# A mixture-of-experts layer on Trainium2: the rows beyond 128 of an expert by plain four-byte products in column tiles, from raw weights

## The reference

```python
scores = sigmoid(xf @ w_router)                 # pick 8 experts of 64 for each token
for each block of rows of one expert e:
    h  = silu(xb @ w_gate[e]) * (xb @ w_up[e])  # 1024 -> 256
    yb = (h @ w_down[e]) * rw                   # 256 -> 1024, weighted
    acc[rows] += yb
shared = (silu(xf @ ws_gate) * (xf @ ws_up)) @ ws_down
x = layer_norm(ALPHA * x + acc + shared)
```

## Time and profile before

| | |
|---|---|
| median of 3 runs | 1641.52 us (1641.01 to 1644.18) |
| the profiled execution | 1632.95 us, its span 1631.3 us |
| TensorE busy | 1574.2 us, 97% of the span |
| DVE, ACT, POOL busy | 73%, 63%, 31% |
| mean granted clock of TensorE | 0.979 |
| DMA | 368.63 MB, mean 226 GB/s |

### The profile page before, as it was taken

One profiled execution on the slowest core, in us unless ns is written; L12 is line 12 of the kernel. 1 busy time (PEld: TensorE's weight loads), 2 busy tenths in 40 slices (PEclk: granted clock), 3 DMA queues, 4 the chain that ended last, 5 costly groups with the idle time before them and its releaser, 6 DMA issues.

```text
span 1631.3 us, 32225 instructions
## 1 busy us (share of the span) xinstructions
PE 1574.2 (97%) x8262; PEld 1310.3 (80%) x8263; DVE 1183.2 (73%) x2038; ACT 1033.3 (63%) x1709; POOL 505.7 (31%) x495
## 2 busy tenths in 40 slices
PE   6999999999999999899999999999999999999987
PEld 6997888888887788788888888788888888888864
DVE  4215777777777788838777888767876787888856
ACT  3215666666666645427667877766776777877855
POOL 0000000000000135532544454543554455454426
PEclk9999999999999999899999999999999999999995
DMA  7223222212223524568999999999998999999987
GB/s 247 91 82 96 67 59 65 71 45 71 58 65 111 185 108 170 196 218 315 318 303 309 304 363 360 329 289 263 331 322 276 286 356 326 348 365 370 366 252 283
DMA packets 161319, 368.63 MB, mean 226 GB/s; under 512 B 53008, under 2 KB 73488, under 8 KB 161264
## 3 DMA queue, kind: packets, MB, share of 16 engines
q1 hardware_dynamic: 136272, 284.21, 49.9%
q0 software_dynamic: 24992, 83.73, 19.8%
HBM read 294.39 MB, written 65.11 MB: 220 GB/s over the span
## 4 chain that ended last, share of the span: by engine, by line
PE 78%; DVE 7%; issue 4%; ACT 3%; DMA 3%; ACTq 2%; POOL 1%; SPq 0%; DVEq 0%; POOLq 0%
PE bank_pair L1032 6%; PE bank_pair L1035 6%; PE bank_pair L1038 6%; PE q_ps L91 4%; PE out_ps L923 4%; PE q_ps L93 4%; PE q_ps L92 4%; PE k_ps L901 4%; PE out_ps L1091 4%; PE out_ps L1092 3%; PE q_ps L1022 3%; PE k_ps L1059 3%; PE k_ps L1060 2%; PE k_ps L1067 2%; DVE gu_lo L1926 2%
## 5 line engine op out<-in xcount | busy, mean ns | idle before, releaser
L1926 DVE TENSOR_TENSOR gu_lo<-raw_gu,gu_hi 128x1024 fp32r<-128x1024 f32 x260 | 306.4, 1219 | 28.7 <-ACT gu_hi L1404 28.7
L1404 ACT CAST gu_hi<-raw_gu 128x1024 fp32r<-128x1024 f32 x260 | 253.3, 1050 | 6.0 <-DMA raw_gu<-in_moe_w_up_dram 6.0
L1032 PE MATMUL bank_pair<-gu_hi,xb_hi 128*128 128x512 f32 x576 | 235.5, 409 | 5.4 <-DVE gu_lo L1926 4.2
L1035 PE MATMUL bank_pair<-gu_lo,xb_hi 128*128 128x512 f32 x576 | 229.1, 398 | 0.0
L689 POOL DMA_INDIRECT sums_scratch<-ys,sidx x63 | 119.8, 1902 | 151.7 <-DMA sums_scratch<-ys,sidx 110.6
L1926 DVE TENSOR_TENSOR dn_lo<-raw_dn,dn_hi 128x1024 fp32r<-128x1024 f32 x130 | 152.6, 1213 | 2.2 <-ACT dn_hi L1404 1.7
L1038 PE MATMUL bank_pair<-gu_hi,xb_lo 128*128 128x512 f32 x576 | 142.7, 390 | 0.0
L1032 PEld LDWEIGHTS bank_pair<-gu_hi,xb_hi 128*128 128x128 f32 x576 | 111.5, 194 | 29.5 <-issue 6.5
L1309 ACT CAST pt_hi<-k_ps 128x512 fp32r<-128x512 f32 (+1 forms) x192 | 85.9, 482 | 74.2 <-PE k_ps L901 73.4
L620 POOL IOTA e<- 128x64 f32 x1 | 0.2, 185 | 426.6 <-DVE xs L1722 426.6
L1404 ACT CAST dn_hi<-raw_dn 128x1024 fp32r<-128x1024 f32 x130 | 130.0, 1051 | 3.2 <-DMA raw_dn<-in_moe_w_down_dram 3.2
(11 more groups left out here) (306 smaller groups left out, 3971.5 us busy)
## 6 DMA issues: line engine op xcount, KB each, us to landing
raw_gu<-in_moe_w_gate_dram SPq DMA_DIRECT2D x128, 512.0 KB, 6.6
raw_gu<-in_moe_w_up_dram SPq DMA_DIRECT2D x128, 512.0 KB, 9.1
raw_dn<-in_moe_w_down_dram SPq DMA_DIRECT2D x128, 512.0 KB, 8.9
wqk<-in_fox_w_in_dram SPq DMA_DIRECT2D x66, 128.0 KB, 2.4
v_scratch<-v_out SPq DMA_DIRECT2D x32, 256.0 KB, 2.8
va<-v_scratch SPq DMA_DIRECT2D x16, 512.0 KB, 4.7
fin<-sums_scratch SPq DMA_DIRECT2D x16, 512.0 KB, 9.0
xs<-in_x_dram SPq DMA_DIRECT2D x8, 512.0 KB, 7.8
```

The lines of the kernel that those rows point to most:

```text
L1032: i = pe.matmul(o3, xb_hi[s][:, c], g_hi[:, :, c], start=c == 0, stop=False, skip_group_check=True)
L1035: pe.matmul(o3, xb_hi[s][:, c], g_lo[:, :, c], start=False, stop=False, skip_group_check=True)
L1404: a.copy(hi, raw).then_inc(S[done], 1)
L1926: dve.tensor_tensor(lo, raw, hi, ALU.subtract).then_inc(S[lo_ok], 1)
```

## The change

The further blocks are multiplied in the plain four-byte type by the raw weights, without split halves. A 32-row block is 32 columns wide as a stationary operand, so four products go to four 32-column tiles of the array, whose results land in partitions 0, 32, 64 and 96 (`x_tile(j)`): for gate/up the tiles are gate and up of the even and of the odd chunks, 16 products of 256 columns; for down they are the two halves of the columns by the two chunks, 4 products of 512 columns. ACT copies and DVE adds the partial sums. `xo` and `ho` are a quarter as wide, and their low halves are gone; so are `hh` (now in `sg`), `gu_x` and `ys2`, which lie in unused partitions of `x_rows2`.

As the further products read the raw weights, these must stay. There is a third raw gate/up buffer; the buffer is `raw_place(s)`. SP waits besides for `started` (gate/up) and `downed` (down). The loops go by six, the least common count of pairs and threes; experts 0, 1, 62 and 63 stand outside. The table `tab` is kept in two-byte integers, cast by POOL from a copy that lies in the third up buffer. Some tiles of the final stage are moved, with three waits for it (`downed` ahead of the sums of tiles 2 to 7, `started` ahead of `tokens`, `c_const` ahead of set 3).

```diff
-            raw_gu = [sb(f"raw_gu{i}", [P, 2, DC, FF], c=m) for i in range(2)]
+            raw_gu = [[sb(f"raw_{n}{i}", [P, DC, FF], c=m) for n in ("gate", "up")] for i in range(2)]
...
+            raw_gu.append([third_gate, sb("raw_up2", [P, DC, FF], c=m)])
...
+        def raw_place(s):
+
+            return s if s < 2 else (0, 2, 1)[(s - 2) % 3]
...
+        ROUND = 6
+        ROUNDS = (E - 4) // ROUND
...
+            def next_gate_up(s, place):
+
+                if place > 3:
+                    sp.wait_ge(S["started"], SH + s - 2)
+                    stand(sp)
+                load_gate_up(place, *(w[ds(s - 1, 1)].rearrange("o k n -> (o k) n") for w in (w_gate, w_up)),
                              lambda k: sp.wait_ge(S["g_lo_ok"], G_PIECES * (s - 2) + k + 1))
 
+            def next_down(s, place):
+                if place > 2:
+                    sp.wait_ge(S["downed"], SH + s - 2)
+                    stand(sp)
+                load_down(place % 2, w_down[ds(s - 1, 1)].rearrange("o k n -> (o k) n"),
                           lambda k: sp.wait_ge(S["d_lo_ok"], D_PIECES * (s - 2) + k + 1))
...
+            sp.wait_ge(S["c_const"], 11)
+            next_gate_up(3, 3)
+            with sp.Fori(0, ROUNDS) as i:
+                for u in range(ROUND):
+                    next_gate_up(ROUND * i + (u + 4), u + 4)
+                    next_down(ROUND * i + (u + 3), u + 3)
...
+            sp.wait_ge(S["downed"], SH + E)
             for t in range(2, TT):
                 load_sums(1, t)
...
+                        g.tensor_copy(tab[:], tab_in).then_inc(S["c_const"], 1)
...
-                for c in range(DC):
-                    pe.matmul(o3, xo[:, c], g_hi[:, :, c], start=c == 0, stop=False, skip_group_check=True)
-                    i = pe.matmul(o3, xo[:, c], g_lo[:, :, c], start=False, stop=c == DC - 1, skip_group_check=True)
+                for c in range(0, DC, 2):
+                    for j in range(4):
+                        i = pe.matmul(out_ps[x_tile(j), BANK:BANK + FF], xo[:, c + j // 2], raw[j % 2][:, c + j // 2], start=c == 0,
+                                      stop=c == DC - 2, skip_group_check=True)
...
-                for r in HALVES:
-                    for c in range(FC):
-                        pe.matmul(out_ps[:, r], ho[:, c], d_hi[:, c, r], start=c == 0, stop=False, skip_group_check=True)
-                        i = pe.matmul(out_ps[:, r], ho[:, c], d_lo[:, c, r], start=False, stop=c == FC - 1, skip_group_check=True)
+                for j in range(4):
+                    c, half = (j // 2, j % 2) if by_rows else (j % 2, j // 2)
+                    i = pe.matmul(out_ps[x_tile(j), BANK:T], ho[:, c], raw[:, c, HALVES[half]], start=True, stop=True, skip_group_check=True)
...
+                a.copy(gu_x[:, 0:FF], out_ps[x_tile(2), BANK:BANK + FF]).then_inc(S["x_half"], 1)
+                a.copy(gu_x[:, FF:2 * FF], out_ps[x_tile(3), BANK:BANK + FF]).then_inc(S["x_up_half"], 1)
...
+                a.copy(y_half, out_ps[2 * XR:P, BANK:T]).then_inc(S["x_y_half"], 1)
...
+                dve.tensor_tensor(gu_x[:, 0:FF], out_ps[x_tile(0), BANK:BANK + FF], gu_x[:, 0:FF], ALU.add).then_inc(S["x_sum"], 1)
...
+                dve.tensor_tensor(ys_x[:, BANK:D], out_ps[x_tile(1), BANK:T], ys_x[:, BANK:D], ALU.add)
+                dve.tensor_tensor(ys_x[:, 0:BANK], out_ps[x_tile(0), BANK:T], y_half[0:XR], ALU.add).then_inc(S["x_scaled"], 1)
```

More of the change, by code:

```diff
@@ L347, in build, with g_piece, d_piece, x_tile @@
         ds = bass.ds
[L349 to L353 removed]
+        def raw_place(s):
+            return s if s < 2 else (0, 2, 1)[(s - 2) % 3]
+        def g_piece(s, k):
+            c = slice((k % 2) * 4, (k % 2) * 4 + 4)
+            return (raw_gu[raw_place(s)][k // 2][:, c], split[s % 2][0][:, k // 2, c], split[s % 2][1][:, k // 2, c])
+        def d_piece(s, k):
+            w = s % 2
             return tuple(a[:, k, :] for a in (raw_dn[w], split[w][2], split[w][3]))
+        def x_tile(j):
+            return slice(j * XR, (j + 1) * XR)
+        ROUND = 6
+        ROUNDS = (E - 4) // ROUND
         def v_bank(n, j, w):
@@ L548, in _ @@
                 elif b == 5:
-                    next_gate_up(2, 0)
+                    next_gate_up(2, 2)
                 elif b == 6:
-                    next_down(2, 0)
+                    next_down(2, 2)
             sp.wait_ge(S["listed"], 16 * TT * TOP_K)
@@ L554, in _ @@
             sp.wait_ge(S["extra_ok"], 2)
-            sp.dma_start(tab[:], tab_dram.rearrange("(p n) o -> p (n o)", p=P)).then_inc(S["c_loads"], 16)
-            next_gate_up(3, 1)
-            with sp.Fori(0, E // 2 - 2) as i:
-                for par in range(2):
-                    next_gate_up(2 * i + (par + 4), par)
-                    next_down(2 * i + (par + 3), 1 - par)
-            next_gate_up(E, 0)
-            next_down(E - 1, 1)
-            next_down(E, 0)
+            sp.dma_start(tab_in, tab_dram.rearrange("(p n) o -> p (n o)", p=P)).then_inc(S["c_loads"], 16)
+            sp.wait_ge(S["c_const"], 11)
[4 more added lines that the diff above has]
+                    next_down(ROUND * i + (u + 3), u + 3)
+            next_gate_up(E, E)
+            next_down(E - 1, E - 1)
+            next_down(E, E)
             def load_sums(j, t):
@@ L1170, in _, with expert @@
                     logits(TT - 1)
-            def expert(e, par, last=False):
+            def expert(e, u, last=False):
+                par = u % 2
                 w = 1 - par
@@ L1224, in expert @@
                 return xi, nx
-            with pe.Fori(0, E // 2 - 1) as i:
-                for par in range(2):
-                    expert(2 * i + par, par)
-            expert(E - 2, 0)
-            expert(E - 1, 1, last=True)
+            for e in range(2):
+                expert(e, e)
+            with pe.Fori(0, ROUNDS) as i:
+                for u in range(2, ROUND + 2):
+                    expert(ROUND * i + u, u)
+            expert(E - 2, E - 2)
+            expert(E - 1, E - 1, last=True)
         @block.scalar
@@ L1522, in load_counts, with expert @@
                 return [act.value_load(earlier[0:1, ds(e + k, 1)], min_val=0, max_val=E * TAB_BLOCKS) for k in range(4)]
-            def expert(e, par, pos, counts):
+            def expert(e, u, pos, counts):
+                par = u % 2
                 m = SH + e
@@ L1597, in _ @@
             expert(1, 1, "", counts)
-            with act.Fori(1, E // 2 - 1) as i:
-                counts = load_counts(2 * i)
-                for par in range(2):
-                    expert(2 * i + par, par, "", counts)
+            with act.Fori(0, ROUNDS) as i:
+                for u in range(2, ROUND + 2):
+                    if u % 2 == 0:
+                        counts = load_counts(ROUND * i + u)
+                    expert(ROUND * i + u, u, "", counts)
             counts = load_counts(E - 2)
-            expert(E - 2, 0, "", counts)
-            expert(E - 1, 1, "last", counts)
+            expert(E - 2, E - 2, "", counts)
+            expert(E - 1, E - 1, "last", counts)
             for t in range(TT):
@@ L2014, in load_counts, with expert @@
                 return [dve.value_load(earlier[0:1, ds(e + k, 1)], min_val=0, max_val=E * TAB_BLOCKS) for k in range(4)]
-            def expert(e, par, counts, last=False):
+            def expert(e, u, counts, last=False):
+                par = u % 2
                 m = SH + e
```

186 lines of the change are left out of this document (93 added, 93 removed).

## The result

The changed kernel takes 1787.04 us (median of 4 runs, 1785.11 to 1792.73) against 1641.76 for the kernel before beside it (4 runs): a ratio of 1.089, 95% interval 1.086 to 1.092. The forecast was 1585, with 0.11 for slower. Its profiled execution has a span of 1785.6 us.

What follows compares the result with a forecast made beforehand. TensorE, busy 97% of the span, was taken as the bound, with DMA limiting short intervals after the change. The stage's -52 us and the ends' -5 made -57: 1576 profiled, 1585 median, range 1550 to 1620.

Steps and rivals of the forecast that it cites:

- Bigger loop bodies: Loops of six experts: fewer branches, 30 to 10, between -10 and +10 us, taken as 0.
- The products: Further gate/up on TensorE in four overlapping column tiles: 1.96 us, 1.68 saved; further down 1.10 us, 0.84 saved; 31 times each.
- own: 15 intervals between turn_h starts holding the expert's own further gate/up: from 14.18 to 12.50 us, TensorE-bound.
- both: 15 intervals holding the previous block's tail and the expert's own block: from 16.56 to 14.04 us, TensorE-bound.
- tail: 15 intervals holding the previous expert's block's turn h and down: TensorE 11.73 to 10.89 us, DMA-bound at 11.95.
- The weights' queue: SP's weight loads, called the deciding step: bursts each interval at 365 GB/s limit the stage's gain to -52 us.
- short interval: 17 intervals between turn_h starts without further block: 9.35 us on TensorE, DMA-bound at 11.6 us, +32.7 in all.
- without carry: Stage sum if no burst may end late into the next interval: -34.7 us; late bursts add about 17.
- The bursts of SP's waits: Rival: weight queue runs dry within each interval, so its mean rate falls; 1640 to 1700 us, chance 0.09.
- Ends: Last intervals and final stage: 4 us off from less DMA backlog, 1 us from the last block.
- small waits pile up: Rival: new small waits, such as POOL's adds, take 1 us from each of 45 intervals; 1605 to 1638, chance 0.13.
- the tiles don't overlap: Rival: TensorE's column tiles queue, further gate/up takes 6.8 us, 4.7 more 31 times; about 1785, chance 0.03.

Runs made afterwards that it cites:

- exact_two_lean: Whole change with loops of two experts (inner loop over raw buffers), TensorE's turn_h and gate_up written once, ahead of the count loads: 1604.31 us, ratio 0.976.
- after_lean_pe: Complete changed kernel, loops of six, with only TensorE's turn_h and gate_up written once, ahead of the count loads: 1675.85 us, ratio 1.019.
- hi_two: Changed kernel with loops of two, further products on split weights' high halves (low halves omitted), no third buffer or new SP waits: 1617.81 us.
- hi_two_lean: hi_two with TensorE's turn_h and gate_up written once, ahead of the count loads and first branch: 1576.81 us, ratio 0.963.
- hi_two_waits: hi_two with the change's two SP waits, for started and downed, left in: 1631.59 us, ratio 0.995.
- loop6_all: Kernel before with only its expert loops changed, from two to six experts a pass on TensorE, DVE, ACT and SP: 1713.14 us, ratio 1.043.
- before_lean_pe: Kernel before with TensorE's turn_h and gate_up written once, ahead of the count loads: 1644.31 us, ratio 1.000.
- hi_four_lean: hi_four with TensorE's turn_h and gate_up written once, ahead of the count loads: 1577.29 us, ratio 0.960.
- hi_four: hi_two with loop bodies of four experts on every engine: 1859.88 us, ratio 1.133.

## Why the prediction was wrong, step by step

**What failed: "Bigger loop bodies: branches fall from 30 to 10, between -10 and +10 us; I take 0".** I counted the branches and not the code. The body of six has 2790 instructions on TensorE (counted in the built program; 1179 in the body of the kernel before) and 669 and 609 on DVE and ACT. In the table, going from exact_two_lean to after_lean_pe adds 83.9 us (71.5 by the medians of the runs): this is the step alone, code loaded while long products are queued. From there to the changed kernel it is 102.8 more. That is not the step alone: it holds the lost cover of the next paragraph, which is 42.8 with loops of two (787.8 less 745.0), and some 60 that the loads cost more where nothing is queued and a copy is jumped over. The trace of before could have given a warning: `q8` carries 28 pieces for a program of 7640 instructions on TensorE (counted likewise), about one for each 273, and none comes between 765 and 1560 us; so code comes once and the loops don't come again.

**A second step that wasn't there.** I let the products shrink by 1.68 us and took everything else as it was. The sequencer's work at the head of each expert was under the last product: 47.1 us of stalls in hi_two, and 41 us won back by hi_two_lean. The sum had no term for it. So even with loops of two, the change in its own order of instructions would come to some 1604 + 40 = 1644 us, an estimate from exact_two_lean and these 41: no gain, and outside the range.

**The products: right.** 1.94 us for 1.96 forecast, and the tiles overlap. In hi_two_lean the medians of `own` and `both` are 12.49 and 14.16 for 12.50 and 14.04. The tail is 11.21 where 10.89 was forecast: 0.52 of 0.84 us saved; I didn't follow this up.

**The weights' queue: right in kind, not the step that decides.** I took 11.6 us for a short interval at 365 GB/s. With loops of two, short intervals have a median of 10.46 in exact_two_lean, whose stage moves 341 GB/s on average:

```profile
745.00:1545.00 800.00, 766.66 (x4477) 585.00 (x4477) 658.93 (x823) 611.23 (x822) 336.43 (x377) 0.99 1.01 341
...
1330.00:1545.00 215.00, 199.19 (x1015) 156.98 (x1014) 172.61 (x205) 161.60 (x204) 78.83 (x87) 0.98 1.02 356
```

The DMA's share is 1.01, as in the earlier trace rows. The 62 intervals are 39.8 us shorter than before; the forecast had -52 with bounds of -35 and -62. In part this agrees by luck: against the forecast without carry, the 17 short intervals and the 15 tails are 19.6 and 6.8 us lower (177.6 for 197.2, 172.5 for 179.3), "own" and "both" 8.9 and 12.3 higher (196.4 for 187.5, 222.9 for 210.6). The bursts of SP's waits, which I gave 0.09 for 1640 to 1700, cost 14 us in hi_two_waits.

**Ends: not shown.** From the last of these `turn_h` to the end of the span it is 77.6 us in the kernel before, 73.9 in the changed one and 74.2 in exact_two_lean: 3.4 to 3.7 off for 5 forecast. But in kernels whose end is that of before it varies as much by itself: 73.0 in loop6_all, 79.6 in before_lean_pe.

So with both steps mended, short bodies and the new order on TensorE, the change is worth 39.5 us of the 57 forecast: exact_two_lean is at 1604.3, inside the range of 1550 to 1620 and beside the case "small waits pile up" (1605 to 1638). That is not the kernel that was forecast; the order alone gained nothing on the kernel before (before_lean_pe). The rival "the tiles don't overlap" gave 1785, within 2 us of the result, and is refuted by the first fence of the timeline: a time that fits is no evidence for its mechanism. None of the rivals held code loading; the chance of 0.11 for slower was for another mechanism.

## What to carry to other kernels

When a change makes a loop's body longer, count its instructions for each engine and look at the page's instruction queues: pieces in proportion to the loop's passes mean that the body no longer stays, and then the engine can stand at each closing branch (5 to 9 us here). A total above that of another kernel isn't enough: look at when the pieces come. Code that is jumped over and never executed also costs, here once, on the first way through. When a change makes an engine's last operation of a loop shorter, look at what its sequencer does behind it (loads of counts, branches), and put that ahead of long work instead. A loop that is unrolled only to name a buffer at build time can keep its short body: an inner loop over the buffers, with a branch around the few operations that touch them.

## What the runs showed of the hardware that I had not expected

Bodies of 1179 and 1568 instructions stayed on TensorE, and one of 1832 of which 1048 were never executed; 1860 and more did not; 446 on VectorE and 406 on ScalarE stayed, 669 and 609 did not (q14 serves both, so the runs don't tell them apart). 283 us lay between 1568 and 1860 (hi_four_lean, hi_four). The longest stalls stand at a loop's closing branch, up to 9.6 us (hi_four), although a piece's own packet takes about 1 us. Over two stalls of 5.39 and 2.27 us TensorE's granted clock was 0.57 on average, from 972 to 984 us of the changed kernel. Four column tiles of plain four-byte products of 256 columns ran in step: a new four records every 0.21 us, and two records to a product.
